# MLP values kept in HBM as one fp32 value, their two parts made after the load

## The reference

```python
hid = jax.nn.relu(jnp.einsum('btd,df->btf', rms_norm(x, norm2_g[l]), w_up[l]))
x = x + jnp.einsum('btf,fd->btd', hid * hid, w_down[l])
```

## Time and profile before

| | |
|---|---|
| median of 3 runs | 2379.39 us (2378.55 to 2379.81) |
| profiled execution | 2377.99 us |
| its span, first to last instruction | 2375.9 us |
| TensorE busy | 2310.4 us, 97% of the span |
| VectorE busy | 1654.5 us, 70% |
| ScalarE busy | 1122.4 us, 47% |
| GpSimd busy (its DMA issues among it) | 383.7 us, 16% |
| moved by DMA | 494.12 MB |
| chain that ended last | TensorE 92%, VectorE 4%, DMA 2% |

### The profile page before, as it was taken

One profiled execution on the slowest core, in us unless ns is written; L12 is line 12 of the kernel. 1 busy time (PEld: TensorE's weight loads), 2 busy tenths in 40 slices (PEclk: granted clock), 3 DMA queues, 4 the chain that ended last, 5 costly groups with the idle time before them and its releaser, 6 DMA issues.

```text
span 2375.9 us, 43945 instructions
## 1 busy us (share of the span) xinstructions
PE 2310.4 (97%) x17246; PEld 2137.9 (90%) x17246; DVE 1654.5 (70%) x2214; ACT 1122.4 (47%) x1735; POOL 383.7 (16%) x653
## 2 busy tenths in 40 slices
PE   8999999999999989699999999999799999999999
PEld 7999999955555659699999999999799999999999
DVE  6355555444444466898888888888588888888887
ACT  6244445533332343455555555655344444444443
POOL 0071000155455410000000000000211111111110
PEclk9999999999999999799999999999899999999999
DMA  6332222699999975145555555555966565555644
GB/s 194 107 96 97 86 94 90 216 350 373 369 375 361 373 299 194 38 164 181 197 204 192 194 189 181 206 198 196 389 219 215 166 223 176 203 193 185 220 165 153
DMA packets 148622, 494.12 MB, mean 208 GB/s; under 512 B 28825, under 2 KB 31514, under 8 KB 137282
## 3 DMA queue, kind: packets, MB, share of 16 engines
q1 hardware_dynamic: 92418, 250.70, 31.2%
q0 software_dynamic: 56000, 240.62, 26.7%
HBM read 412.33 MB, written 78.91 MB: 207 GB/s over the span
## 4 chain that ended last, share of the span: by engine, by line
PE 92%; DVE 4%; DMA 2%; issue 1%; ACT 1%; POOL 0%; SPq 0%; DVEq 0%; ACTq 0%; POOLq 0%
PE bank L2583 19%; PE bank L2586 19%; PE bank L2579 19%; PE bank L570 14%; PE bank L575 7%; PE bank L2470 4%; PE bank L2445 3%; PE bank L2405 2%; DMA hid_in<-hid_parts 1%; PE bank L2347 1%; DMA w_raw<-weights 1%; PE bank L2247 1%; PE bank L2376 1%; PE bank L2453 1%; PE bank L2361 1%
## 5 line engine op out<-in xcount | busy, mean ns | idle before, releaser
L570 PE MATMUL bank<-x_act,w_hi 128*128 128x364 f32 (+1 forms) x1728 | 377.3, 329 | 0.7 <-DVE w_lo L561 0.6
L2579 PE MATMUL bank<-hid_in,down_ring 128*128 128x272 f32 x1792 | 280.9, 289 | 15.3 <-issue 8.4
L2583 PE MATMUL bank<-hid_in,down_ring 128*128 128x272 f32 x1792 | 280.4, 289 | 0.0
L2586 PE MATMUL bank<-hid_in,down_ring 128*128 128x272 f32 x1792 | 279.9, 288 | 0.0
L2579 PE MATMUL bank<-x_op,ring 128*128 128x272 f32 x1792 | 264.0, 290 | 16.1 <-ACT x_op L1168 10.9
L570 PEld LDWEIGHTS bank<-x_act,w_hi 128*128 128x128 f32 x1728 | 275.1, 188 | 2.2 <-DVE w_lo L1584 1.0
L2583 PE MATMUL bank<-x_op,ring 128*128 128x272 f32 x1792 | 264.3, 290 | 2.3 <-DVE x_op L2104 2.3
L2586 PE MATMUL bank<-x_op,ring 128*128 128x272 f32 x1792 | 263.2, 289 | 0.0
L2579 PEld LDWEIGHTS bank<-hid_in,down_ring 128*128 128x128 f32 x1792 | 247.2, 189 | 15.7 <-issue 8.6
L1168 ACT ACTIVATE lines<-bank 128x272 f32<-128x272 f32 x240 | 95.6, 398 | 349.1 <-PE bank L2586 349.1
L2579 PEld LDWEIGHTS bank<-x_op,ring 128*128 128x128 f32 x1792 | 240.9, 190 | 17.5 <-issue 17.5
(11 more groups left out here) (300 smaller groups left out, 3605.9 us busy)
## 6 DMA issues: line engine op xcount, KB each, us to landing
up_raw<-w_up SPq DMA_DIRECT2D x128, 512.0 KB, 4.1
hid_parts<-hid_out POOLq DMA_DIRECT2D x32, 1904.0 KB, 6.5
w_raw<-weights SPq DMA_DIRECT2D x43, 1024.0 KB, 4.8
down_raw<-w_down SPq DMA_DIRECT2D x128, 320.0 KB, 3.8
hid_in<-hid_parts POOLq DMA_DIRECT2D x62, 544.0 KB, 4.8
v_ring<-sb_v POOLq DMA_DIRECT2D x128, 256.0 KB, 5.3
v_ring<-fox_v POOLq DMA_DIRECT2D x120, 256.0 KB, 4.8
hid_in<-hid_parts POOLq DMA_DIRECT2D x93, 272.0 KB, 6.8
```

The lines of the kernel that those rows point to most:

```text
L570: ins = nc.tensor.matmul(bank[:, base + b, 0:n], hi, row[:, t:t + n], start=begin, stop=end)
L2579: mm(out, part_of(n, 0)[:, cols], operand(k)[:, 0], start=(first and k == 0), stop=False, skip_group_check=True)
L2583: mm(out, part_of(n, 0)[:, P * k:P * k + P], operand(k)[:, 1], start=False, stop=False, skip_group_check=True)
L2586: ins = mm(out, part_of(n, 1)[:, P * k:P * k + P], operand(k)[:, 0], start=False, stop=(k == last), skip_group_check=True)
```

## The change

`hid_out` becomes two buffers `hid_f`, each of the seven values alone, without parts; the store moves 952 KB. The first five tiles go to a tensor of their own, `hid_early`, in the order in which they are loaded; the others to `hid_parts`. `hidden_high` and `hidden_low` are gone. On the way down each load brings the value into the low half of its place; ScalarE copies the high part beside it (`high_first`, `high_hidden`) and GpSimd subtracts in place (`low_first`, `low_hidden`), for P2, P5 and P4 of the first tiles VectorE does (its `low_first`). TensorE waits for the low parts in place of the loads. Unit 31's squares wait for the store of unit 29, not 30; the store of unit 30 moves behind six other steps of GpSimd.

```diff
 def store_hidden(u):
-    pool.wait_ge(*hid_ready.at(u + 1))
-    pool.dma_start(hid_parts[u], hid_out[:].bitcast(F32)).then_inc(hid_stored, 16)
+    pool.wait_ge(*hid_mixed.at(u + 1))
+    if u:
+        pool.wait_ge(hid_stored, 16 * u)
+    to = hid_early[:, :, u].rearrange("o p n -> p o n") if u < FIRST_TILES else hid_parts[u - FIRST_TILES]
+    pool.dma_start(to, hid_f[u % 2][:]).then_inc(hid_stored, 16)
...
+def low_hidden(i):
+    pool.wait_ge(*hid_hi.at(7 + 5 * (i - FIRST_TILES + 1)))
+    for r in range(len(hid_in)):
+        low = hid_in[r][:, :, 1, i % HID_SLOTS]
+        nc.gpsimd.tensor_tensor(low, low.bitcast(F32), hid_in[r][:, :, 0, i % HID_SLOTS].bitcast(F32), ALU.subtract
+                                ).then_inc(hid_lo.s, 1)
...
 for u in range(LAST - 1):
     store_hidden(u)
-for o in (P1, P2, P6, P5):
+for o in range(7):
     load_first(o)
-store_hidden(LAST - 1)
-for o in (P7, P4, P3):
-    load_first(o)
+    if o in (P5, P4):
+        low_first(o - 3)
 load_rows(0)
 load_hidden(FIRST_TILES)
+low_first(P7)
+low_first(P3)
+store_hidden(LAST - 1)
+low_hidden(FIRST_TILES)
+store_hidden(LAST)
 load_rows(1)
-store_hidden(LAST)
 load_hidden(FIRST_TILES + 1)
+low_hidden(FIRST_TILES + 1)
...
 for i in range(HID_SLOTS, HID_LOADS):
     load_hidden(i)
+    low_hidden(i)
...
-            if v:
-                act.wait_ge(hid_stored, 16 * v)
-            f(hid_f[:, 0:7:6], ends_a[:], ACT.Square).then_inc(a_squared.s, 1)
+            if v >= 2:
+                act.wait_ge(hid_stored, 16 * (v - 1))
+            f(hid_f[v % 2][:, 0:7:6], ends_a[:], ACT.Square).then_inc(a_squared.s, 1)
...
+        HIGH_FIRST = {AT[UP_UNITS - 1, o] + 3: o for o in range(7)}
+        HIGH_HIDDEN = {AT[UP_UNITS, P5]: FIRST_TILES, AT[UP_UNITS + 1, P5]: FIRST_TILES + 1}
+        for i in range(HID_SLOTS, HID_LOADS):
+            HIGH_HIDDEN[AT[UP_UNITS + user_of(i - HID_SLOTS), P3] + 3] = i
...
-            if o == P6 and 1 <= v <= UP_UNITS:
-                hidden_high(v - 1)
+            if n in HIGH_FIRST:
+                high_first(HIGH_FIRST[n])
+            if n in HIGH_HIDDEN:
+                high_hidden(HIGH_HIDDEN[n])
...
+            if u == UP_UNITS:
+                pe.wait_ge(*(first_lo if o in (P2, P5, P4) else hid_lo).at(o // 2 + 1))
+            elif u > UP_UNITS and o == P1:
+                pe.wait_ge(*hid_lo.at(4 + 5 * (k0 + depth(u) - FIRST_TILES)))
```

More of the change, by code:

```diff
@@ L291, in build_step @@
     lines = at("lines", [P, 3, HALF], F32, A_LINES)
-    hid_out = at("hid_out", [P, 7, 2, HALF], F32R, A_HID)
-    hid_h, hid_f = hid_out[:, :, 0], hid_out[:, :, 1].bitcast(F32)
+    hid_f = [at(f"hid_f{i}", [P, 7, HALF], F32, A_HID + 7 * HALF * 4 * i) for i in range(2)]
     ends_b = at("ends_b", [P, 2, HALF], F32, A_HID + 14 * HALF * 4)
@@ L1117, in load_first, with low_first @@
             r, a = IN_AT[o]
+            pool.wait_ge(hid_stored, 16 * FIRST_TILES)
             pool.wait_ge(*product_done.at(AT[LAST, o] + 1))
-            pool.dma_start(hid_in[r][:, a, 0:FIRST_TILES].bitcast(F32),
-                           hid_parts[0:FIRST_TILES, :, o].rearrange("q p i n -> p q i n")).then_inc(first_in[o], 16)
+            pool.dma_start(hid_in[r][:, a, 1, 0:FIRST_TILES].bitcast(F32), hid_early[o]).then_inc(first_in[o], 16)
+        def low_first(o):
+            r, a = IN_AT[o]
+            pool.wait_ge(*hid_hi.at(o + 1))
+            low = hid_in[r][:, a, 1, 0:FIRST_TILES]
+            nc.gpsimd.tensor_tensor(low, low.bitcast(F32), hid_in[r][:, a, 0, 0:FIRST_TILES].bitcast(F32), ALU.subtract
+                                    ).then_inc(hid_lo.s, 1)
         def load_hidden(i):
@@ L2142, in mix_hidden, with low_first @@
         def mix_hidden(u):
+            hf = hid_f[u % 2]
             dve.wait_ge(*a_squared.at(u + 1))
             dve.wait_ge(*b_squared.at(2 * u + 2))
-            v.tensor_tensor(hid_f[:, P5], ends_b[:, 0], hid_f[:, P1], ALU.subtract).then_inc(hid_first.s, 1)
-            v.tensor_tensor(hid_f[:, P7], hid_f[:, P3], ends_b[:, 0], ALU.subtract).then_inc(hid_first.s, 1)
+            v.tensor_tensor(hf[:, P5], ends_b[:, 0], hf[:, P1], ALU.subtract).then_inc(hid_first.s, 1)
+            v.tensor_tensor(hf[:, P7], hf[:, P3], ends_b[:, 0], ALU.subtract).then_inc(hid_first.s, 1)
             dve.wait_ge(*hid_first.at(2 * u + 1))
-            v.tensor_tensor(hid_f[:, P6], hid_f[:, P3], hid_f[:, P5], ALU.subtract).then_inc(hid_second.s, 1)
+            v.tensor_tensor(hf[:, P6], hf[:, P3], hf[:, P5], ALU.subtract).then_inc(hid_second.s, 1)
             dve.wait_ge(*hid_second.at(u + 1))
[L2150 to L2154, removed]
+            v.tensor_tensor(hf[:, P4], hf[:, P2], hf[:, P6], ALU.subtract).then_inc(hid_mixed.s, 1)
+        def low_first(o):
+            r, a = IN_AT[o]
+            dve.wait_ge(*hid_hi.at(o + 1))
+            low = hid_in[r][:, a, 1, 0:FIRST_TILES]
+            v.tensor_tensor(low, low.bitcast(F32), hid_in[r][:, a, 0, 0:FIRST_TILES].bitcast(F32), ALU.subtract
+                            ).then_inc(first_lo.s, 1)
+        LOW_FIRST = {AT[UP_UNITS - 1, o] + 4: o for o in (P2, P5, P4)}
         def join_a(u):
@@ L2182, in _ @@
                 op_low_part(n + RING)
+            if n in LOW_FIRST:
+                low_first(LOW_FIRST[n])
             if o == P1:
```

40 lines of the change are left out of this document (22 added, 18 removed).

## The result

| | before | changed |
|---|---|---|
| median | 2378.97 us (2378.14 to 2379.81) | 2454.44 us (2448.29 to 2456.7) |
| ratio | | 1.0312, 95% interval 1.0299 to 1.0325 |
| span of the profiled execution | 2375.9 us | 2446.6 us |
| moved by DMA | 494.12 MB | 427.86 MB |

The changed kernel is 3.1% or 75 us slower, although it moves 66 MB less. The forecast was no difference, 2380.9 us, with a range of 2370 to 2398. The time lies outside it. The profiled execution is the fastest of the four (2448.29 us), so the spans are 70.7 us apart where the medians are 75.5 apart.

What follows compares the result with a forecast made beforehand. TensorE was taken as the bound, busy throughout with gaps only at the turn. Up 0, turn -3.5 and down +5 gave +1.5 us on 2379.4, so 2380.9 us, no tellable difference; range 2370 to 2398.

Steps and rivals of the forecast that it cites:

- Up, 0 us: Way up: ScalarE copies and VectorE subtractions taken away gain nothing, since TensorE has no gap there; 0 us.
- The turn, -3.5 us: Way up to way down: unit 33 starts 6.6 us earlier, less 1.6 and 1.5 us of losses; bounds -10 and 0.
- take turns: GpSimd and VectorE subtracting together: they alternate by instruction, with 0.14 us given back at a hand-over.
- Down, ScalarE: Way down: five copies a tile, 2.2 us, and 0.4 us of waiting for the load, inside P3's 1.5 us to spare.
- Latency ... for double the bytes; I take 4: Way down: a tile's halved loads land in 4 us, against an earlier median of 6.0.
- Its five issues begin 0.46 us after the last product on the old tile: Way down: GpSimd starts a tile's load issues then, the last of them some 2.5 us later.
- third rival: Way down: loads land too late for ScalarE, `ends_a` 0.9 us late for P3 in 29 units; +26 us, 2402, chance 0.11.
- Down, GpSimd and VectorE: Way down: two bursts, 7.6 us, fit VectorE's 8.5 us idle in three units; +5 us, bounds 0 and +22.
- The sum: Whole kernel: -3.5 at the turn and +5 in the way down give +1.5 us, 2380.9 us.
- second rival: Way down: VectorE becomes the bound, a burst costing it more than 4.2 us; +22, 2398 us, chance 0.24.
- Gaps of a microsecond or more in every unit: Sign in TensorE's way down that the forecast is wrong: second rival if VectorE or GpSimd ends them, third if a load.
- VectorE's busy share near 97%: Sign in the way down that the forecast is right, beside VectorE subtractions of 640 elements at 1.3 to 2 us.

Runs made afterwards that it cites:

- both stalls of the way down removed: Changed kernel with ScalarE's copies two products later and GpSimd's subtractions of tiles 7 to 35 on 8 of 272 columns: 2376.73 us, ratio 0.9988.
- all-VectorE kernel: Changed kernel with ScalarE's copies two products later and all low parts subtracted by VectorE, GpSimd only issuing DMAs: 2372.82 us, ratio 0.9974.
- thin weights: Changed kernel, but from unit 38 on every weight load brings 64 of its 640 or 768 columns: 2406.07 us, ratio 1.0114.
- 8 columns: Changed kernel with GpSimd's subtractions of tiles 7 to 35 on 8 of 272 columns, ScalarE's copies left in place: 2408.74 us, ratio 1.0126.
- copies two products later: Changed kernel with ScalarE's five copies of a tile two products later, subtractions whole on GpSimd: 2397.75 us, ratio 1.0078.

## Why the prediction was wrong, step by step

**Up, 0 us: right.** Both kernels have 4310 matmuls in 540 us. The copies and subtractions taken from there were covered.

**The turn, -3.5 us: right in size, its parts less so.** Unit 33 starts at 1703.94 (forecast 1701.5, bounds 1698 and 1707) behind a GpSimd subtraction, and the kernel with both stalls of the way down removed is 2.4 us faster than before. The start of unit 33 wins 4.2 us where 6.6 were forecast, and the losses behind it, put at 3.1, were not measured by themselves. GpSimd's price for 1360 elements, 3.4 us, was near: 3.1 for each of two. One detail was wrong. The forecast let the two engines take turns everywhere. Here two GpSimd subtractions run back to back, and VectorE's addition gets in behind neither:

```profile
1685.34 7.29 DVE L2102 TENSOR_TENSOR down_sum<-down_raw,down_sum 128x640 f32<-128x640 f32 x1
```
```profile
1685.74 6.19 POOL L1128 TENSOR_TENSOR hid_in<-hid_in 128x1360 fp32r<-128x1360 f32 x2
```

That addition takes 0.82 us in the kernel without GpSimd's subtractions (1686.78 above). It delays P4's low part, hence the 7.40 us before P4. It also reaches unit 33: ScalarE waits 4.32 us for its result before the high part at 1692.72, tile 5's copies stand behind that, and GpSimd idles 3.16 us until 1695.60 before tile 5's subtractions, where the forecast had it busy without a break and starting them at 1694. That this is most of the 3.7 us by which the all-VectorE kernel comes to unit 33 sooner is argued from the rows and not run by itself.

**Down, ScalarE: the step that failed first.** "Latency ... for double the bytes; I take 4" was the term. The last load takes 6.6 us. The loads of the earlier trace rows were read as one group with one median, and the halving was applied to all of it; but the last one, which alone decides, owes its time to the weights that SyncE issues beside it: with thin weights it is 4.6 at most. A second term failed with it. "Its five issues begin 0.46 us after the last product on the old tile" holds for the first tile of a pair only; for the second, GpSimd is still subtracting, and the issues leave 3.5 us later. The forecast used GpSimd's serial queue at the turn and left it out here. The third rival had the late load at a chance of 0.11 and a price of +26; alone it measures +32.0 (8 columns against both taken away). The nearness is partly luck: the rival let P3 be 0.9 us late in all 29 units, and it is 1.4 late in every second one. The price of the five copies themselves, 2.2 us, was right: 2.17.

**Down, GpSimd and VectorE: the burst's price right, what it costs the kernel four times too small.** The forecast put a burst at 3.1 to 3.8 us of VectorE's time, and it is 3.28. It then set two bursts, 7.6 us, against 8.5 us of VectorE's idle time in three units and got 0.3 us of stall, +5 in all. With the copies two products later it is +21.0. Two bursts of 3.28 fit into the 8.5, and into the 7.2 that VectorE's 464.15 busy us of 560 in the earlier trace rows leave of three units. What failed is the use of that sum: it was taken from VectorE's load, as if its idle time lay where it could be used, and with every load on time. In the kernel with the later copies part of it lies in front of the burst, here the second of a pair:

```profile
1845.96 1.22 DVE L2073 TENSOR_TENSOR down_ring<-down_sum,down_ring 128x768 fp32r<-128x768 f32 x1 [2.01 <-ACT down_ring L1192]
1847.11 2.13 DVE L2102 TENSOR_TENSOR down_sum<-down_raw,down_sum 128x768 f32<-128x768 f32 x1
1849.16 0.71 DVE L2178 TENSOR_TENSOR ends_b<-lines,bank 128x544 f32<-128x544 f32 x1
```

VectorE idles 2.01 us for a high part of weights, because ScalarE waits 1.73 us for the load, issued behind the first burst, and makes the tile's five copies (1842.75 to 1844.92) first. The same copies release GpSimd's burst. So the idle time comes just before the rows that are then slowed, and P7 at 1850.51 waits 0.42 us for the line behind `ends_b`. The first bursts of the pairs, whose loads are on time, have no gap before their P7. The burst lies two products later here than the forecast had it, and ScalarE waits for every second tile's loads (22.3 us in 12 times, where the kernel with 8 columns as well has none): 21.0 us is the price of the subtractions at that place with these waits among it, and not of the shared time alone.

**The sum: costs taken one by one.** The second and third rival stood as cases that exclude each other, each with the rest of the kernel on time. The third came true. The second did not as it was stated: its condition is a burst over 4.2 us and a full VectorE, and the burst is 3.28 with VectorE at 86%; that its +22 is near the 21.0 is luck. But bursts and late loads meet in one chain: the copies that wait for the load also release the subtractions and hold the line that VectorE waits for, and the subtractions hold back the next tile's loads. Of the 77.7 us, 24.7 lie in that. No case in the forecast added them; +26 and +22 added to the turn would have reached 2424.

**Its tests pointed the right way.** "Gaps of a microsecond or more in every unit (second rival if VectorE or GpSimd ends them, third if a load does)" is near what the profile shows: 1.7 us and 1.1 us in the burst above, one ended by VectorE after a load's wait, one by the line behind VectorE's sum. They did not part the two rivals, since the load ends neither gap directly. "VectorE's busy share near 97%" is 86%.

## What to carry to other kernels

Time the last transfer of a group by itself, and by what other queues issue beside it: a wait for a group is a wait for its slowest member, and half the bytes need not mean half the time (here 6.2 to 5.0 us for the loads among the weights). Before work goes to GpSimd to spare VectorE, compare what it costs VectorE there with what it costs VectorE to do it: here 3.28 us against 2.3. Look also at what stands behind the new work in that engine's queue: here the next tile's loads left 3.5 us late. And when one instruction both waits for a late input and releases other work, add the delays along the chain and count an engine's idle time only where it lies: idle time in front of a burst does not pay for it.

## What the runs showed of the hardware

- Two GpSimd subtractions of 1360 elements back to back (6.19 us) held a VectorE addition of 640 elements for 7.29 us through both, though its row starts 0.40 us before theirs, while in the bursts of 272 and 544 elements the engines took turns (VectorE's 0.82 us rows at 1.16 to 1.99).
- A 136 KB load by GpSimd's queue landed in 6.6 us with three 384 KB weight loads of SyncE's issued around it; with these cut to 64 columns no load took over 4.6. The minimum, 3.0 and 2.9, hardly moved.
- GpSimd issued five loads right behind its five subtractions (1935.33, behind a row of 7.11 us from 1928.29), 5.95 us after the start of the product that freed their place; with the subtractions at 0.88 us a tile it was 2.42.
- VectorE ran at 92% of 560 us with one TensorE wait of 0.7 us for it, when it did the subtractions itself; at 91% with GpSimd subtracting beside it and every second tile's loads late (506.86 us), TensorE waited in 15 places for the line behind it.
